# Who makes the high part of the output projection's weights: GpSimd or ScalarE

## What is computed

```python
merged = jax.nn.sigmoid(g_a) * br_a + jax.nn.sigmoid(g_b) * br_b + jax.nn.sigmoid(g_c) * br_c
return merged @ w_o
...
h_lat = _layer_norm(alpha * h_lat + gate[:, None, :] * out_lat, post_ln_g[l], post_ln_b[l])
```

## Time and profile before

| | before |
|---|---|
| time, median of three runs | 2757.2 us |
| time of the profiled execution | 2757.11 us |
| its span in the profile | 2755.3 us |
| TensorE busy | 2672.7 us (97% of the span) |
| GpSimd busy | 1021.2 us (37%) |
| ScalarE busy | 841.1 us (31%) |
| output projection, first layer | jobs 0 to 15, about 1379 to 1503 us |
| output projection, second layer | jobs 0 to 15, about 2624 to 2725 us, and the norm's end after it |

### The profile page before, as it was taken

One profiled execution on the slowest core, in us unless ns is written; L12 is line 12 of the kernel. 1 busy time (PEld: TensorE's weight loads), 2 busy tenths in 40 slices (PEclk: granted clock), 3 DMA queues, 4 the chain that ended last, 5 costly groups with the idle time before them and its releaser, 6 DMA issues.

```text
span 2755.3 us, 32885 instructions
## 1 busy us (share of the span) xinstructions
PE 2672.7 (97%) x13578; PEld 2196.3 (80%) x13578; DVE 1585.6 (58%) x1512; ACT 841.1 (31%) x1220; POOL 1021.2 (37%) x915
## 2 busy tenths in 40 slices
PE   7999999999999999999999899999999999999996
PEld 4888888888887888888878688888888888877874
DVE  3745544541018888847657763555552299866756
ACT  3234444442100000034314423545552000005313
POOL 3721111112224333334575662111114355554573
PEclk9999999999999999999999999999999999999998
DMA  6111111111255111124333512101112211114433
GB/s 264 35 60 35 39 35 39 35 41 62 76 188 212 44 38 39 39 90 149 133 128 126 173 41 69 43 35 35 39 43 81 77 46 47 46 58 145 142 124 113
DMA packets 75892, 224.74 MB, mean 82 GB/s; under 512 B 8672, under 2 KB 12000, under 8 KB 74720
## 3 DMA queue, kind: packets, MB, share of 16 engines
q1 hardware_dynamic: 53280, 182.26, 19.3%
q10 hardware_dynamic: 22464, 40.38, 3.9%
HBM read 177.52 MB, written 45.09 MB: 81 GB/s over the span
## 4 chain that ended last, share of the span: by engine, by line
PE 88%; DVE 6%; ACT 3%; issue 2%; DMA 1%; POOL 0%; SPq 0%; ACTq 0%; DVEq 0%; POOLq 0%
PE PS L733 48%; PE PS L864 20%; PE PS L900 6%; PE PS L922 5%; PE PS L909 5%; PE PS L932 1%; ACT Pr L1205 1%; DVE cv L1683 1%; PE PS L776 1%; DVE e L1756 1%; DMA wmA<-wmod 1%; ACT PTh L1228 1%; PE PS L782 1%; PE PS L886 0%; DMA wraw<-w 0%
## 5 line engine op out<-in xcount | busy, mean ns | idle before, releaser
L622 POOL CAST wh<-wraw 128x512 fp32r<-128x512 f32 (+1 forms) x424 | 333.7, 787 | 1262.8 <-PE PS L733 630.6
L624 POOL TENSOR_TENSOR wl<-wraw,wh 128x512 fp32r<-128x512 f32 (+1 forms) x424 | 611.2, 1441 | 34.0
L1650 DVE TENSOR_TENSOR PTl<-PS,PTh 128x512 fp32r<-128x512 f32 x328 | 226.9, 692 | 417.6 <-ACT PTh L1228 417.5
L733 PE MATMUL PS<-Uh,wh 128*128 128x512 f32 (+1 forms) x1536 | 428.8, 377 | 15.3 <-issue 9.6
L1683 DVE SCALAR_TENSOR_TENSOR cv<-hc,vec,cv 128x1024 f32<-128x1024 f32 x360 | 435.8, 1238 | 8.8
L733 PE MATMUL PS<-Uh,wl 128*128 128x512 f32 (+1 forms) x1536 | 420.4, 371 | 0.0
L733 PE MATMUL PS<-Ul,wh 128*128 128x512 f32 (+1 forms) x1536 | 418.7, 370 | 0.0
L864 PE MATMUL PS<-Uh,wh 128*128 128x512 f32 (+1 forms) x960 | 358.7, 374 | 2.8 <-POOL wl L624 2.3
L864 PE MATMUL PS<-Uh,wl 128*128 128x512 f32 (+1 forms) x960 | 357.1, 372 | 0.0
L864 PE MATMUL PS<-Ul,wh 128*128 128x512 f32 (+1 forms) x960 | 356.9, 372 | 0.0
L1228 ACT ACTIVATE PTh<-PS 128x512 fp32r<-128x512 f32 x328 | 196.2, 598 | 438.8 <-PE PS L909 434.2
(11 more groups left out here) (159 smaller groups left out, 3446.3 us busy)
## 6 DMA issues: line engine op xcount, KB each, us to landing
wraw<-w SPq DMA_DIRECT2D x164, 512.0 KB, 3.4
graw<-stg ACTq DMA_DIRECT2D x88, 256.0 KB, 2.0
wmB<-wmod SPq DMA_DIRECT2D x32, 512.0 KB, 5.7
e<-graw SPq DMA_DIRECT2D x24, 640.0 KB, 3.9
wraw<-w SPq DMA_DIRECT2D x48, 256.0 KB, 4.1
e<-graw SPq DMA_DIRECT2D x24, 512.0 KB, 3.6
wmA<-wmod SPq DMA_DIRECT2D x8, 1024.0 KB, 12.3
hL<-hT_in SPq DMA_DIRECT2D x8, 640.0 KB, 21.1
```

Of the source, the lines that this page charges most:

```text
L622: nc.gpsimd.tensor_copy(wh[par][:, s], wraw[par][:, s]).then_inc(whi[par], 1)
L624: nc.gpsimd.tensor_tensor(wl[par][:, s], wraw[par][:, s], wh[par][:, s].bitcast(F32), ALU.subtract).then_inc(wsplit[par], 1)
L733: ins = mmul(PS[:, at + c:at + c + m], w[par][:, k * P:(k + 1) * P], x[:, k, c0 + c:c0 + c + m], start=(first and a == 0), stop=(last and ...
L1650: tt(PTl[b][:], PS[:, PT0[bank]:PT0[bank] + 512], PTh[b][:].bitcast(F32), ALU.subtract).then_inc(pt_free[bank], 1)
```

## The change

For the 512-column jobs of the output projection from job 2 of a layer on (jobs 2 to 7 of the first layer, jobs 2 to 15 of the second; 20 jobs in all) the cast to the high part leaves GpSimd, which keeps the two subtractions. ScalarE makes the two casts of job n+2 inside `scaled` of job n: after it has seen job n done and before it copies job n's result out. It waits there for the weights of job n+2 to have landed.

In the second layer ScalarE's squares of group 0 are also laid out differently: squares 0 and 1, `scaled` of job 8, squares 2 to 4, `scaled` of job 9, squares 5 to 7, `scaled` of job 10. In the first layer the order of the squares stays.

```diff
--- before.py
+++ after.py
@@ -132,6 +132,12 @@
 
 def is_gate(n):
     return tile_of(n)[1] < 0 or I_G <= tile_of(n)[1] < I_ZA
+
+
+def cast_by_act(n):
+
+    l, i = tile_of(n)
+    return I_OUT + 2 <= i < (NJ if l + 1 == DEPTH else I_OUT + KD)
 
 
 def jobs_of(n):
@@ -619,7 +625,8 @@
                         wait_job(pool, n - 2)
                 for a in range(2):
                     s = slice(a * w // 2, (a + 1) * w // 2)
-                    nc.gpsimd.tensor_copy(wh[par][:, s], wraw[par][:, s]).then_inc(whi[par], 1)
+                    if not cast_by_act(n):
+                        nc.gpsimd.tensor_copy(wh[par][:, s], wraw[par][:, s]).then_inc(whi[par], 1)
                     pool.wait_ge(whi[par], nh * 2 + (a + 1))
                     nc.gpsimd.tensor_tensor(wl[par][:, s], wraw[par][:, s],
                                             wh[par][:, s].bitcast(F32), ALU.subtract).then_inc(wsplit[par], 1)
@@ -1360,10 +1367,19 @@
                 if l == 0:
                     act.wait_ge(s_mod, 5)
 
+                def cast(n):
+                    par = n % 2
+                    act.wait_ge(wland[par], n // 2 * 16 + 16)
+                    for a in range(2):
+                        x = slice(a * D // 2, (a + 1) * D // 2)
+                        fn(wh[par][:, x], wraw[par][:, x], ACT.Copy).then_inc(whi[par], 1)
+
                 def scaled(g, j):
                     n = j0 + I_OUT + g * KD + j
                     c0, w = group(l, g)
                     wait_job(act, n)
+                    if tile_of(n + 2)[0] == l and cast_by_act(n + 2):
+                        cast(n + 2)
                     if j >= 2:
                         act.wait_ge(s_z, KD * (2 * l + g) + j - 1)
                     for a, m, who in segs(T):
@@ -1417,10 +1433,12 @@
                 for j in range(KD):
                     scaled(0, j)
                 mean(O_OMEAN[0], KD)
-                group_squares(0, range(4))
+                some, more = (4, KD) if nxt else (2, 5)
+                group_squares(0, range(some))
                 scaled(1, 0)
-                group_squares(0, range(4, KD))
+                group_squares(0, range(some, more))
                 scaled(1, 1)
+                group_squares(0, range(more, KD))
                 if nxt:
                     root(O_OVAR[0], KD)
                     scaled(1, 2)
```

## The result

The changed kernel takes 2777.54 us (median of 4 runs, 2775.79 to 2778.46), the kernel before in the same measurement 2757.23 us. The ratio is 1.0071 with an interval of 1.0055 to 1.0087: **0.7% slower, 20.3 us**. Slower was forecast, by 8.1 us; the time lies above the stated range of 2758.5 to 2770.5. The profiled execution took 2778.46 us; its span is 2776.6 us, 21.3 us more than before.

What follows compares the result with a forecast made beforehand. TensorE was taken to bound the kernel (88% of the chain that ended last). Losses of 2.6 us in the first layer and 5.5 in the second, 8.1 together, on 2757.11 us gave 2765.2 us, range 2758.5 to 2770.5.

Steps and rivals of the forecast that it cites:

- The loop: Output projection, both layers: cast, copy, z_sum, residual load, weights request, landing, next cast; 6.72 us against TensorE's 5.58 per job.
- the sum: One loop turn's terms, 6.72 us; over the kernel, losses of 2.6 (first layer) + 5.5 (second) = 8.1 us.
- 2.2 us from cast to matmul: Output projection: TensorE needs about 2.2 us from the start of a cast to its first matmul.
- the reserve: Output projection: slack before lateness reaches TensorE, 5.58 - 2.2 = 3.4 us, lasting about three jobs.
- One sign: Jobs 2 to 7: job 7 would be 4 to 5 us late in its cast, 2 to 3 us in its end.
- I give this 0: VectorE beside GpSimd: fewer GpSimd instructions change nothing, 0 us, as VectorE will wait for ScalarE in this stretch.
- the steps from cast to request: Within one loop turn: casts and copy 1.06, z_sum 0.78, residual load 0.71, weights request 0.37; 2.92 us.
- The reserve swallows it: Rival, both layers: landings at 3.62 us or shorter shrink the loss to 4.1 us or less; 2761.2 or less, chance 0.18.
- not slower: Rival: earlier slots, less GpSimd-VectorE conflict, waits of jobs 11, 12, 15 (3.4 us) go; 2753.8 to 2757, chance 0.07.
- Heavier loss: Rival: landings of 4.5 us (first layer) and 6.89 (job 15), or lower TensorE clock before job 15; 2770 and more, chance 0.12.

Runs made afterwards that it cites:

- the two cuts: Changed kernel with ScalarE's casts placed behind the copy of the result: 2753.61 us, 0.9998; changed kernel with weights requested ahead of the residual tile: 2751.23 us, 0.9989 to before.
- time only: Changed kernel with ScalarE making two spare copies of the result, not waiting for weights, and GpSimd casting: 2759.21 us, 1.0015 to the kernel before.
- casts only: Changed kernel with the second layer's squares in their old order, casts still on ScalarE: 2773.14 us, 1.0067 to the kernel before.
- wait only: Changed kernel with ScalarE still waiting for job n+2's weights but casting nothing, GpSimd casting as before: 2765.99 us, 1.0041 to the kernel before.
- first layer alone: Changed kernel with ScalarE's casts only in the first layer's jobs 2 to 7, squares in the old order: 2761.28 us, 1.0024 to the kernel before.

## Why the prediction was right in kind and wrong in size

**Right, and now shown.** The loop closes, with about the 6.72 us per turn of the sum. Where the weights landed 3.6 to 3.9 us after their request, the casts stood 6.71 us behind the last ones in the first layer and 6.66, 6.77, 6.73 and 6.89 us in the second; where they took 4.0 to 4.6 us, 7.0 to 7.6 us. A pair of casts costs 1.06 us up to the copy, and 2.2 us from cast to matmul was met (2667.11 to 2669.34). In the second layer the reserve held for about three jobs. That request and wait make the loss is shown by the two cuts, which lose nothing with all the casts on ScalarE. By them, too, the casts taken off GpSimd were worth nothing that can be told. That a delay without the wait makes a small part of it at most (4.2 of 20 us) is shown by "time only". One sign came out larger than stated: job 7 of the first layer, counted from job 0 on, was 6.6 us late in its casts (4 to 5 forecast) and 3.5 us in its end (2 to 3).

**Step that failed: terms put at nothing.** The mechanism was right and the sum too small. It priced VectorE's operations beside GpSimd's subtractions as if they ran alone ("I give this 0"), and took TensorE's clock as unchanged behind the new waits. The first layer was put at 2.6 us and lost 7.4, the second at 5.5 and lost 12.7. Worked out from the traces, each from job 0 on:

- *First layer, up to job 8 (+2.1).* Job 7's casts came 35.3 us after the first ones, not 33.6, and job 8 started 4.7 us late. Of the 2.1 us, 0.8 are job 1's slower clock (7.52 us to job 3's casts, the loop gave 6.72). Another 0.7 are the five landings behind it, which took 3.67, 3.67, 4.17, 4.09 and 4.13 us where the sum had 3.80. The last 0.6 are the steps from cast to request, 3.02 to 3.05 us instead of 2.92, with z_sum at 0.80 to 0.83 us instead of 0.69. Beside two of the three slower landings no more data moved than beside the faster ones (some 800 KB), so what made them slower is open.
- *First layer, the norm (+1.4) and the clock (about 1.4).* Prediction: what follows job 8 is only shifted. But VectorE's operations fell on other work of GpSimd's than before. The first two deviations took 2.40 us instead of 1.29, beside the split of job 9, and the last two additions of squares 2.76 us instead of 1.70. VectorE's timeline of the changed kernel, then of the kernel before:

```profile
1441.19 2.40 DVE L1874 TENSOR_TENSOR Z<-Z,e 128x512 f32<-128x512 f32 x2 [3.55 <-ACTq L1307]
...
1454.65 2.76 DVE L1774 TENSOR_TENSOR e<-e,e 128x512 f32<-128x512 f32 x2
```

```profile
1435.49 1.29 DVE L1856 TENSOR_TENSOR Z<-Z,e 128x512 f32<-128x512 f32 x2 [1.95 <-ACTq L1300]
...
1448.62 1.70 DVE L1756 TENSOR_TENSOR e<-e,e 128x512 f32<-128x512 f32 x2
```

  Steps between them became 0.6 us shorter, and the wait for the variance grew from 0.92 to 2.30 us. It is 2.30 us, with these two durations, in the four profiles whose first layer has the loop (changed kernel, casts only, wait only, first layer alone), and 0.91 or 0.92 in all ten others, the two with the casts ahead and the weights asked for first among them. Then the pair of matmuls took 2.07 us: TensorE's granted clock had fallen.
- *Second layer, up to the mean (+2.7).* Up to job 7's result this is 1.1 us: the steps from cast to request took 3.00 to 3.04 us instead of 2.92 each, and job 8's weights took 4.61 us, with job 9's asked for 2.1 us behind them. From job 7's result to the sum for the mean it is 1.6 us: the casts of jobs 8 and 9 and their four subtractions followed each other, and VectorE worked beside them. ScalarE's, then VectorE's timeline of the changed kernel:

```profile
2639.94 1.15 ACT L1375 ACTIVATE wh<-wraw 128x512 fp32r<-128x512 f32 x2 [3.74 <-PE PS L740]
...
2681.61 1.15 ACT L1375 ACTIVATE wh<-wraw 128x512 fp32r<-128x512 f32 x2 [5.88 <-DMA wraw<-w]
...
2683.49 1.16 ACT L1375 ACTIVATE wh<-wraw 128x512 fp32r<-128x512 f32 x2 [0.16 <-DMA wraw<-w]
```

```profile
2684.25 1.67 DVE L1866 TENSOR_TENSOR e<-e,Z 128x512 f32<-128x512 f32 x1
2685.96 1.64 DVE L1859 SCALAR_TENSOR_TENSOR Z<-e,e 128x512 f32<-128x512 f32 x1
2687.63 1.63 DVE L1866 TENSOR_TENSOR e<-e,Z 128x512 f32<-128x512 f32 x1
```

  Three operations at 1.64 us in a row, where I had 0.69 for two of them. The sum for the mean came 49.4 us after job 0, forecast 46.7.
- *Second layer, the clock (1.5).* Behind the 3.23 us wait TensorE ran at the lower level into job 8: 3.1 us from the sum to the fourth matmul behind it, instead of 1.7. The prediction had a fallen clock only as a risk ahead of job 15.
- *Second layer, to job 15 (about 3).* VectorE's chain from the casts of job 10 to z_sum of job 8 took 3.8 us, not 3.0, and from those of job 11 to z_sum of job 9 6.1, not 5.2, each with one addition of 1.61 us beside a subtraction of GpSimd's. Job 13's landing took 4.9 us. Job 15's took 5.24; 5.0 had been taken.
- *Behind job 15 (0, by luck).* The prediction has this part keep its length. It did so because two falls of TensorE's clock cancelled. Behind the 2.42 us wait ahead of job 15 the granted clock fell to 0.50 from about 2741 to 2744 us, and the way from job 15's start to the next sum over the channels became 1.55 us longer (2740.15 to 2749.86, against 2718.86 to 2727.02). Behind that sum the clock had been low in the trace before and was not in the changed one, and the rest of the span became 1.54 us shorter. In the fourteen profiles the two matmuls of that sum took anything from 1.12 to 2.08 us, so this gain is not the change's. TensorE's timeline of the kernel before, then of the changed kernel:

```profile
2727.02 2.08 PE L782 MATMUL PS<-e,ones 128*128 128x512 f32 x2 [2.35 <-DVEq L1850]
```

```profile
2749.86 1.13 PE L789 MATMUL PS<-e,ones 128*128 128x512 f32 x2 [2.34 <-DVEq L1868]
```

Read this way, the longer operations of VectorE make about 6 of the 12 us by which the sum fell short, the clock a little under 4 and the landings about 2. So one sentence carried about half of the error: "I give this 0, as VectorE will wait for ScalarE". VectorE did wait. But the landing that ends ScalarE's wait sets off GpSimd's subtractions too, 0.8 us later by way of the first cast, and the operations that VectorE has to do behind the copy fall on them.

**Rivals.** "The reserve swallows it" and "not slower" are out. The first had its estimate of 3.2 us for a landing from the Trainium skill (DMA: Bandwidth & Descriptors, Anatomy of one DMA). That section gives its formula for DMAs issued through GpSimd, while these go through SyncE's queue; no landing read here took under 3.6 us. "Heavier loss" is nearest by its time, but its chance was 0.12 and its reasons came true in part only. The landings were 3.67 to 4.17 us in the first layer (it had 4.5) and 5.24 us for job 15 (it had 6.89). The clock did fall in the wait ahead of job 15, as it had it, but what it cost the total was lost behind the waits for the first layer's variance and the second layer's mean, where it had no term. What these kernels leave open is the exact share of the collisions, the clock and the landings: they were read from one trace and not varied by themselves. The two profiled executions also differ by up to 1.5 us in single places for reasons of their own: 1.15 us before the first cast, job 1's clock, and the clock behind job 15 the other way.

## What to carry to other kernels

Before an engine is given a wait for a DMA, follow the request back: if it stands in some queue behind the work that the engine does after the wait, the wait is on a circle, and its whole length (transfer, issue and all steps between) has to be less than the time of the jobs that it spans (here one), not just less than the reserve. Such a loss costs the difference at every turn once the reserve is gone, and it is undone by moving the request or the wait, while the moved work can stay. And in the length of the circle every operation is to be priced beside its neighbours, since one event that starts two engines can make them collide at every turn, as it did here.

## What was not expected of the hardware

- z_sum on VectorE took 1.73 us beside a subtraction on GpSimd that had started 0.1 us before it, and 0.69 us alone. The Trainium skill (SBUF — State Buffer, Summary: rules for kernel authors) says that of a VectorE operation with two SBUF inputs and a GpSimd operation that reads SBUF the second to issue waits until the first is done. By it z_sum would end 0.69 us after the end of the 1.29 us subtraction, 1410.12 + 1.29 + 0.69 = 1412.10, and the trace has 1411.95: it agrees within 0.15 us. The prediction took this lock as speaking for a gain; here it worked against the change.
- TensorE's granted clock fell to a mean of 0.57 to 0.66 behind waits of 2.3 to 3.2 us, in stretches of 4 to 5 us. Windows of the changed kernel (us, busy us of TensorE, its weight loads, VectorE, ScalarE and GpSimd, granted clock, DMA share, GB/s):

```profile
1457.00:1462.00 5.00, 4.47 (x14) 3.08 (x15) 4.72 (x4) 1.33 (x2) 2.74 (x2) 0.66 0.44 147
2689.00:2693.00 4.00, 3.63 (x7) 2.21 (x8) 1.17 (x3) 0.78 (x2) 0.00 (x0) 0.57 0.00 0
```

  It does not fall each time, and not always at once. Behind the same 2.30 us wait the pair of matmuls took 2.07 us here and 1.91 with the first layer alone, and with the casts only it took 1.12 us and the clock stayed at 1.00. In "wait only" the pair took 1.13 us at a clock of 1.00, and the clock fell to 0.50 about 1 us later, from about 1454 to 1457.5 us. So the length of the first matmuls alone does not tell what a wait cost in clock.
